# A gated recurrence by products of gates folded level by level, and the first two tiles' merge in its stage

## The reference, cut to what matters

```
def gla_chunk(S, q, k, v, g):
    C = q.shape[2]
    cum = jnp.cumsum(g, axis=2)
    inter = jnp.einsum('bhtc,bhcv->bhtv', q * jnp.exp(cum), S)
    diff = cum[:, :, :, None, :] - cum[:, :, None, :, :]
    decay = jnp.where(causal, jnp.exp(jnp.where(causal, diff, 0.0)), 0.0)
    A = jnp.einsum('bhtc,bhsc,bhtsc->bhts', q, k, decay)
    intra = jnp.einsum('bhts,bhsv->bhtv', A, v)
    last = cum[:, :, -1]
    S_new = (jnp.exp(last)[..., None] * S
             + jnp.einsum('bhsc,bhsv->bhcv', k * jnp.exp(last[:, :, None, :] - cum), v))
    return S_new, inter + intra

q = silu(rq); f = lb + (1 - lb) * sigmoid(rf); k = 1 - f; g = log(f)   # 4 heads, 128 features, 528 tokens
o = rmsnorm(o, norm_w) * silu(rg)
x = x + concat(att, o) @ w_out
```

## Time and profile before

| | us |
|---|---|
| median of three runs | 3038.01 |
| the profiled execution, its own time | 3036.15 |
| its span in the profile | 3034.3 |
| the recurrence, 291.06 to 393.54 | 102.5 |
| the first merge, 393.85 to 440.68 | 46.8 |
| the norm behind it, 441.0 to 454.16 | 13.2 |

### The profile page before, as it was taken

How to read it: one execution, slowest core, us unless ns; L and a number is a source line. 1 busy time by engine, 2 the same in 40 slices (tenths; PEclk the granted TensorE clock), 3 DMA queues, 4 the chain that set the end, 5 groups by cost and what they waited for, 6 DMA issues and landing times. The chain is left out here.

```text
span 3034.3 us, 32474 instructions
## 1 busy us (share of the span) xinstructions
PE 2652.2 (87%) x11426; PEld 1813.3 (60%) x11426; DVE 1893.7 (62%) x3864; ACT 1289.7 (43%) x2806; POOL 669.0 (22%) x638
## 2 busy tenths in 40 slices
PE   6988768898889877789999999699798697999998
PEld 6877647334444332245555555499686455788887
DVE  5786836777777677777777776555554655343323
ACT  3234223544444344555656655344234245232222
POOL 2210000434443433444444434100000020000000
PEclk9998788999999999999999999899898699999999
DMA  6752024999999999999999999656130101222332
GB/s 214 277 183 61 1 97 162 411 413 406 420 420 421 405 404 422 419 412 419 419 412 412 408 415 415 238 186 194 65 94 28 37 22 49 98 70 97 98 99 75
DMA packets 131731, 750.81 MB, mean 247 GB/s; under 512 B 17408, under 2 KB 17936, under 8 KB 65248
## 3 DMA queue, kind: packets, MB, share of 16 engines
q0 software_dynamic: 81824, 575.43, 46.7%
q1 hardware_dynamic: 49744, 173.30, 16.5%
HBM read 746.57 MB, written 2.10 MB: 247 GB/s over the span
## 5 line engine op out<-in xcount | busy, mean ns | idle before, releaser
L1646 PE MATMUL peer_y<-rows,diag 128*128 128x512 f32 x2048 | 995.2, 613 | 178.0 <-ACT diag L1626 166.3
L1600 DVE CUSTOM_DVE_ANT_0 rows<-rows,hidden 128x1024 f32<-128x1024 f32 x512 | 627.8, 1226 | 375.6 <-DMA rows<-in_peer_table,experts 370.4
L1587 POOL DMA_INDIRECT rows<-in_peer_table,experts x512 | 587.8, 1148 | 1042.5 <-PE peer_y L1646 799.2
L1646 PEld LDWEIGHTS peer_y<-rows,diag 128*128 128x128 f32 x2048 | 363.1, 192 | 592.2 <-ACT diag L1626 301.3
L1623 ACT ACTIVATE hid<-hid 128x1 f32<-128x1 f32 x512 | 102.6, 200 | 544.1 <-DVE hid L1600 540.7
L2249 DVE TENSOR_TENSOR piece_w_low<-piece_raw,piece_w_high 128x1024 fp32r<-128x1024 f32 x132 | 161.1, 1222 | 102.4 <-ACT piece_w_high L2244 102.2
L1626 ACT ACTIVATE diag<-ident,hid 128x128 f32<-128x128 f32 x512 | 205.6, 401 | 16.7
L2244 ACT ACTIVATE piece_w_high<-piece_raw 128x1024 fp32r<-128x1024 f32 x132 | 138.6, 1052 | 108.2 <-PE out_bank L152 77.6
L1624 ACT ACTIVATE hid<-hid,gates 128x1 f32<-128x1 f32 x512 | 150.8, 295 | 16.6
L417 ACT ACTIVATE proj_w_high<-proj_raw 128x1024 fp32r<-128x1024 f32 (+2 forms) x57 | 57.5, 1012 | 217.1 <-PE proj_pair L152 116.9
L150 PE MATMUL peer_y<-peer_feat_high,early_w_high 128*128 128x256 f32 x352 | 144.5, 410 | 2.0 <-issue 2.0
(11 more groups left out here) (522 smaller groups left out, 5637.1 us busy)
## 6 DMA issues: line engine op xcount, KB each, us to landing
ada<-in_w_ada POOLq DMA_DIRECT2D x96, 384.0 KB, 4.4
piece_raw<-in_ffn_w_gate SPq DMA_DIRECT2D x44, 512.0 KB, 3.5
piece_raw<-in_ffn_w_up SPq DMA_DIRECT2D x44, 512.0 KB, 4.4
piece_raw<-in_ffn_w_down SPq DMA_DIRECT2D x44, 512.0 KB, 3.4
query_raw<-in_peer_w_query SPq DMA_DIRECT2D x32, 512.0 KB, 6.6
early_raw<-in_ffn_w_gate SPq DMA_DIRECT2D x22, 512.0 KB
early_raw<-in_ffn_w_up SPq DMA_DIRECT2D x22, 512.0 KB, 14.4
early_raw<-in_ffn_w_down SPq DMA_DIRECT2D x22, 512.0 KB, 7.8
```

The lines of the kernel that those rows point to most:

```text
L1587: pool.indirect_dma_start(self.rows[:, b, :], None, self.table, bass.IndirectOffsetOnAxis(ap=self.experts[:, unit % self.SETS, n % TOPK:n ...
L1600: dve.tensor_tensor_reduce(out=self.rows[:, b, 0:D], in0=self.rows[:, b, 0:D], in1=self.hidden[:, tile, :], scale=1.0, scalar=0.0, op0=ALU ...
L1646: last = pe.matmul(self.y[self.bank(tile)][:, c * BANK:(c + 1) * BANK], self.diag[:, b, :], self.rows[:, b, D + c * BANK:D + (c + 1) * BAN ...
```

## The change

`gated_scan` and `first_merge(half=0)` become one stage, `scan_and_merge`.

The gates are no longer turned into logarithms. The levels now go from the finest to the coarsest, and keys and queries are changed in place. Level 0 multiplies keys by plain queries, level 1 keys by queries times their gate; after each further level the second half of each block pair of the queries is multiplied by the product of the gates of the first half (`fold`, on VectorE), and the first half of the keys by the product of the gates of the second (on GpSimd). The products themselves come by halving (`next_gain`). Masks are now "at least so far apart", and a coarser level overwrites a finer one. From level 5 on ScalarE copies the blocks from PSUM without a mask. Tiles go in two chunks of 256 tokens, each with waits of its own. Logarithm, exponentials, running sums, `differences` and `weighted` are gone.

The merge of tiles 0 and 1 follows in the same stage: the attention half's squares, sums, root and scaling stand beside the levels, and `w_out` is loaded at the stage's start. The one-column sums of the modulation and what VectorE makes of them move into `peer_features(half=0)`, as the class `Modulation`.

```
+        qe = room.sbuf("qe", [P, RH, T])
+        gain = [t.fm[:, AH:2 * AH, :]]
+        for j in range(1, LV + 1):
+            gain.append(room.sbuf(f"gain{2 ** j}", [P, RH, (NT if j <= 4 else T) // 2 ** j])[:, :, :])
...
+            pool.wait_ge(keys_ready, 1)
+            for j in range(LV - 1):
+                if j:
+                    pool.wait_ge(gained, j)
+                for c in range(2):
+                    lo, hi = (0 if c == 0 and j <= 3 else NM + c * CHUNK), NM + (c + 1) * CHUNK
+                    own = halves(k[:, :, lo:hi], 2 ** j, False)
+                    back = 0 if j <= 4 else NM
+                    pool.wait_ge(l_done, (j + 1) * TT + 2 * c + 2)
+                    pool.tensor_tensor(own, own, gains(j, lo - back, hi - back, True), ALU.mult).then_inc(folded_keys, 1)
...
+            move_gate(0)
+            move_gate(1)
+            act.wait_ge(ms_ready, 1)
+            act.activation(ss[:, :, 0:4], ss[:, :, 0:4], ACT.Sqrt).then_inc(rstd_ready, 1)
+            for u in range(2, 6):
+                move_gate(u)
+            for n in range(TT):
+                kept(OPEN, n)
             move_keys(0)
+            for c in range(2):
+                kept(LV - 1, 2 * c)
+                kept(LV - 1, 2 * c + 1)
+                last_halves(c)
+            kept(LV, 0)
+            kept(LV, 1)
             move_keys(1)
+            move_keys(2)
+            kept(LV, 2)
+            kept(LV, 3)
+            move_keys(3)
+            for n in range(2):
                 act.wait_ge(o_summed, n + 1)
+                act.activation(t.rec[:, n, :], o_bank[n], ACT.Copy)
+                act.activation(sq[:, n * BANK:(n + 1) * BANK], o_bank[n], ACT.Square).then_inc(squared, 1)
...
+            def fold_queries(j, c):
+                b, lo, hi = 2 ** j, c * CHUNK, (c + 1) * CHUNK
+                own = halves(qe[:, :, lo:hi], b, True)
+                return dve.tensor_tensor(own, own, gains(j, real_at(j) + lo, real_at(j) + hi, False), ALU.mult)
+
+            def fold(j, c):
+                dve.wait_ge(l_done, (j + 1) * TT + 2 * c + 2)
+                fold_queries(j, c).then_inc(folded, 1)
...
+            def next_gain(j):
+
+                own = gain[j][:, :, 1:] if j == 4 else gain[j]
+                two = own.rearrange("p h (m w) -> p h m w", w=2)
+                dve.tensor_tensor(gain[j + 1], two[:, :, :, 0], two[:, :, :, 1], ALU.mult).then_inc(gained, 1)
+                dve.wait_ge(gained, j + 1)
...
+            for lv in range(OPEN):
+                for c in range(2):
+                    kept(lv, 2 * c)
+                    kept(lv, 2 * c + 1)
+                    if lv >= 1:
+                        fold(lv - 1, c)
+                next_gain(lv)
+                if lv == 0:
+                    mean_squares(0)
+                if lv == 1:
+                    dve.wait_ge(rstd_ready, 1)
+                    for i in range(2):
+                        last = normed(0, i)
+                    last.then_inc(scaled, 1)
+            for j in (OPEN - 1, OPEN):
+                for c in range(2):
+                    fold(j, c)
+                    if j == OPEN:
+                        fold_last_keys(c)
+                if j == OPEN - 1:
+                    next_gain(OPEN)
+                    next_gain(OPEN + 1)
+                    next_state(0)
+            for c in range(2):
+                fold_last_queries(c)
+            for m in range(1, TT):
+                next_state(m)
+            mean_squares(1)
...
+            for lv in range(LV):
+                for n in range(TT):
+                    level(lv, n)
+                if lv < 4:
+                    gate_row(2 + lv)
+                if lv == OPEN:
+                    turn_keys(0)
+                    state_sums(0)
+            level(LV, 0)
+            level(LV, 1)
             turn_keys(1)
+            turn_keys(2)
+            level(LV, 2)
+            level(LV, 3)
+            state_sums(1)
+            turn_keys(3)
+            state_sums(2)
+            state_sums(3)
             for n in range(TT):
                 outputs(n)
+            pe.wait_ge(scaled, 3)
...
+class Modulation:
...
+    def sums(self, pe):
+        pe.wait_ge(self.ones_ready, 2)
+        for part, pair_of in enumerate(self.PARTS):
+            for a, m in enumerate(pair_of):
+                for f in range(KC):
+                    col = m * D + f * P
+                    last = pe.matmul(self.cols[:, part, a, f:f + 1], self.t.ada_acc[:, col:col + P], self.ones[:, 0:1],
+                                     start=True, stop=True)
+        last.then_inc(self.done, 1)
...
@@ peer_features, TensorE, behind the four groups of transposes @@
+            if modulation is not None:
+                modulation.sums(pe)
             beside.sums(pe, END)
```

More of the change, by code:

```diff
@@ L1036, in _ @@
-            dve.wait_ge(apart_ready, 1)
-            for lv in range(LV + 1):
-                last = dve.tensor_scalar(inside[:, lv, :], apart[:, :], float(2 * HALVES[lv] if lv < LV else 1), None,
-                                         ALU.is_lt)
-            last.then_inc(masks, 1)
-            dve.wait_ge(logs, 1)
-            chain.link(dve.tensor_scalar(k, k, -1.0, 1.0, ALU.mult, ALU.add))
-            for h in range(RH):
-                last = dve.tensor_tensor_scan(cum[:, h, :], keep[:, :], cum[:, h, :], 0.0, ALU.mult, ALU.add)
-                last.then_inc(cum_done, 1) if h == RH - 1 else chain.link(last)
@@ L1105, in _ @@
[L1105 to L1111 removed]
+            dve.wait_ge(sigmoids, 1)
+            for h in range(RH):
+                last = dve.tensor_scalar(gain[0][:, h, :], t.fm[:, K + h, :], t.one_lb[:, h:h + 1], t.lb[:, h:h + 1],
+                                         ALU.mult, ALU.add)
@@ new lines, in _ @@
+            dve.wait_ge(rstd_ready, 2)
+            dve.wait_ge(gates, 1)
+            for i in range(2):
+                chain.link(normed(1, i))
+                dve.tensor_tensor(t.rec[:, i, :], t.rec[:, i, :], t.rg[:, i, :], ALU.mult).then_inc(scaled, 1)
+            for u in range(4):
+                tile, c = u // 2, u % 2
+                dve.wait_ge(out_done, u + 1)
+                x = t.x[:, tile, c * BANK:(c + 1) * BANK]
+                dve.tensor_tensor(x, x, turn_bank[u], ALU.add)
@@ new lines, in _ @@
+            pe.wait_ge(moved, KC)
+            pe.wait_ge(w_loaded, 32)
+            for u in range(4):
+                i, c = u // 2, u % 2
+                for f in range(KC):
+                    last = pe.matmul(turn_bank[u], feat[:, f, i * P:(i + 1) * P], w_out[:, c, f, :],
+                                     start=(f == 0), stop=(f == KC - 1))
+                last.then_inc(out_done, 1)
+        for name, n in (("squared", 4), ("ms", 2), ("rstd", 2), ("gates", 1), ("scaled", 3), ("turned", 4), ("moved", KC),
+                        ("out_done", 4)):
+            Signal(core, f"merge_{name}").used(n)
@@ L1210, in part_of @@
             return (t.mixed if part == 0 else t.rec)[:, 2 * half + i, :]
-        if half == 0:
-            @block.sync
-            def _(sp):
-                for c in range(2):
-                    sp.dma_start(w_out[:, c, :, :], dram["w_out_t"][c]).then_inc(w_loaded.handle, 16)
         @block.gpsimd
@@ L1303, in _ @@
             beside.sums(pe, END)
-        for s, n in ((w_loaded, 32 * (half == 0)), (squared, 4), (sums, 2), (ms_ready, 1), (rstd_ready, 1), (gates, 1),
+        for s, n in ((squared, 4), (sums, 2), (ms_ready, 1), (rstd_ready, 1), (gates, 1),
                      (scaled, 4), (turned, 4), (moved, KC), (out_done, 4)):
@@ L1386, in _ @@
             beside.dots(dve, END)
+            if modulation is not None:
+                modulation.move(dve, chain)
         @block.tensor
@@ L3272, in half_of @@
                 keys_in = Signal(core, "keys_in")
-                peer_features(core, t, dram, half, half_feat, norm_room, e.hidden, row_w, beside, weights, keys, keys_in)
+                modulation = Modulation(core, t, dram, small, e.y[0]) if half == 0 else None
+                peer_features(core, t, dram, half, half_feat, norm_room, e.hidden, row_w, beside, weights, keys, keys_in,
+                              modulation)
                 peer_scores(core, t, dram, half, half_feat, weights, keys, keys_in, query, scores, beside, e)
```

372 lines of the change are left out of this document (193 added, 179 removed).

## The result

The changed kernel takes 2994.97 us (median of 4 runs, 2991.26 to 2997.85). The kernel before, run beside it on the same chip, takes 3037.48 us. The ratio is 0.9862, with a 95% interval from 0.9847 to 0.9876, so 42.5 us less. Forecast were 2998 us and 40 us less.

A forecast was written before the change was run, and what follows sets the result against it. VectorE's hand-written order was taken to pace the old levels and TensorE the merge, with stages in series. Gain 54.5, less 4 for GpSimd and 10.5 for modulation, gave 40 us less: 2998 us, range 2984 to 3018.

The forecast's parts named there:

- lock included: Levels: GpSimd's folds hold VectorE operations through the shared port pair, 4 us against the gain, bounds 0 and 18.
- the walk: Step-by-step timing of the new recurrence and merge stage on the old profile's clock: ends at 386.2, not 440.7, gain 54.5 us.
- 4 us of held operations: Levels: VectorE's folds, gains and attention-half scalings may wait until GpSimd's folds are through; 4 us against.
- The rival with a low clock throughout: Levels and outputs: TensorE's clock stays low, some 20 us more, 3018 us; chance 0.07.
- The price on VectorE: Levels: GpSimd's folds delay four of ten VectorE folds and one pair of scalings; 4 us, bounds 0 and 18.
- the operations named: Levels: four of VectorE's ten folds and one pair of scalings, hit by 0.3 to 1.4 us each.
- The rival of an exclusive port as the bound: Levels: GpSimd's and VectorE's folds exclude each other, or a fold takes 2.8 us; 3012, with both 3016; chance 0.17.
- the middle value: Merge: passes by `w_out` and last addition take 29.5 us, between 28.7 at full clock and the earlier 30.7.
- The modulation: Norm stage: 96 one-column passes behind the transposes, only 6.8 us covered; 10.5 us against, bounds 4.6 and 14.5.
- The picture of fast passes first and slow ones behind: Norm stage: 40 one-column passes at 0.115 us in 4.6 us, then the clock falls and 56 run at 0.215.
- given back later: Later stages: the gain is lost if one waits for something with a time of its own; chance 0.01.

The follow-up runs named there:

- the folds in part: Changed kernel, but each of GpSimd's twelve key folds multiplies only one block of one head, leaving out nearly all key folding; 2991.13 us, ratio 0.9865 to the kernel before.
- the merge apart: Changed kernel, but the first two tiles' merge is again its own stage behind the recurrence, with the attention half's norm in it; 2997.74 us, ratio 0.9889.

## Why the prediction was right

**The recurrence.** Its outputs were forecast to begin 38.7 us earlier, lock included; it was 39.4 in the mean. The first masked copy came 9.5 us into the stage (forecast 9.8), level 0 was through at 16.6 (16.5). TensorE ended level 5 at 40.3, where the walk's 36.3 and its 4 us of held operations give the same. That is luck in part: 1.6 of it is the low clock in level 3, and in the other two profiles the level ended at 38.7. There the held operations cost 3.7 (35.0 with the folds in part), and the walk without them was 1.3 too long. From there to the outputs it took 15.8 (15.4), which again holds 1.6 us of low clock that the walk didn't have. The copies come 0.65 us apart and a fold takes 0.67, with 0.59 to the next operation, as taken from the earlier trace rows. ScalarE's block copies, estimated between the earlier trace rows, took 0.23, 0.28 and 0.38 us for 0.22, 0.28 and 0.43. Behind level 0 the clock cost more than the nothing put down for it: 1.6 us in the 48 passes of levels 6 and 7, and 1.6 in level 3 in one profile of three. The rival with a low clock throughout is out, as the levels took 0.117 a pass but for the one.

**GpSimd.** A fold was put at 1.5 us between 1.2 and 2.8. It takes 1.11 to 1.21 when nothing holds it, at or under the lower bound, and up to 1.59 when something does. The price on VectorE was put at 4; the kernel with the key folds left out in part shows 3.7 to 4.2. The bounds of 0 and 18 were wide enough to hold nearly anything, but the operations named (four folds and the pair of scalings) are the ones that were held; of what was held, only L1079 with its 1.06 us is of a kind that the prediction didn't name. The rival of an exclusive port as the bound (3012 to 3016) is out: the 16 masked copies took 0.70 to 0.74 us each, with folds beside many of them, and 0.71 to 0.74 before the change with none. The Trainium skill ("SBUF — State Buffer", section "SBUF: two separate sides") says that the later of the two waits for the whole instruction of the other. The trace agrees on both sides. The first scaling started at 311.25 beside a fold that ran from 311.02 to 312.44, and it ended 0.54 us behind the fold where it takes 0.69 by itself. A fold of GpSimd that started at 328.76, just behind one of VectorE that ran from 328.72 to 329.41, ended 0.94 us behind that one where it takes 1.11 by itself.

What the prediction didn't ask is whether GpSimd is worth it. In the changed kernel it hardly is: all folds on VectorE give 2993.69, the same within the spread.

**The merge.** From the outputs to its end 41.9 us (43.3). The passes by `w_out` ran all at the full clock and took 28.5 with the last addition; I had taken the middle value, 29.5.

**The modulation.** This is the term that was too small. Forecast 10.5 us, with bounds of 4.6 (4.8 by its own terms) and 14.5; it cost 13.5, 14.1 and 11.3 in the three profiles, 13.0 in the mean. There are two parts. The passes took 17.8, 18.3 and 15.5 us, where 16.6 were forecast (17.2 in the mean). The picture of fast passes first and slow ones behind is right: clock 0.91 from 396.4 to 400 and 0.50 from there to the end. The other part was missing: the norm's transposes ahead of them took 5.47 us in all three, and not the 3.84 of the earlier trace rows, partly at the low clock after the same 3.7 us of idleness. That is 1.6 of the 2.5 us. They ran in 3.84 before and in three of the experiments' profiles, in 5.47 in four, and in 6.6 in two; why isn't settled.

**The sum.** -39.4 for the recurrence, -13.2 for the merge and +13.0 for the modulation give the -39.7 (-39.6 by the rounded terms), against a forecast of -38.7, -11.8 and +10.5. So the sum is closer than its terms, which is luck: the modulation's 2.5 too little was made up by 0.7 and 1.4 too little gain. The 3 us beyond it are those of the experts' part that no step of the prediction covers. Nothing was given back later: the first gather starts 40 us earlier from the stage's start.

What paid was the algorithm. With the merge apart, the folded recurrence alone begins its outputs 45.2 us earlier than before. The common stage then adds 3 us by the split and 4 by the medians.

## What to carry to other kernels

When an edit removes a long preparation, ask what was hidden under it. Here 20 us of one-column sums had cost nothing, and cost 13 us behind the norm or 15 at the start once their cover was gone; cut up, most of them fit into waits that TensorE had anyway.

In a loop where two engines have nearly the same time for a round, nothing is free to put "beside" it. The attention half's sums and scalings on VectorE cost 5 us in the levels, and nothing measurable behind them. Work handed to GpSimd paid 1.2 us here where VectorE set the pace and was held by it, and 3.5 where the levels went at TensorE's pace with GpSimd's folds and at VectorE's without them. VectorE's folds were held there too (one took 1.63 us), but TensorE's 4.55 us a level hid it.

## What the runs showed of the hardware that was not expected

- A VectorE operation on 8 columns with one tensor input took 1229 ns beside a GpSimd fold and 173 alone. I had looked for holding only in operations with two inputs in SBUF. The same section of the Trainium skill names, beside these, a mode of VectorE that uses both ports; which mode this operation ran in no run here shows. Masked copies out of PSUM were never held (0.70 to 0.74 us).
- The holding goes both ways. GpSimd's folds of 512 elements took 1.11 to 1.15 us beside masked copies and 1.50 to 1.59 when VectorE worked on two SBUF tiles. The Trainium skill ("GPSIMD Engine Reference", section "Elementwise — side-by-side cycle accounting") has 4497 ns for 2048 elements, from which I had estimated 1.2 for a fold of 544. The trace has 1.15 and 1.21 for the ones beside masked copies.
- One-column passes kept TensorE busy from end to end and the granted clock fell under them all the same, from a mean of 0.91 up to 400.0 to 0.50 from there on. In three profiles of one kernel 96 of them took 15.5, 17.8 and 18.3 us. At the stage's start, they took 20.64, as before the change.
- The granted clock also fell to 0.50 and rose again inside the 48 passes of levels 6 and 7, with TensorE busy from end to end. They took 7.25 us in six profiles and 5.62 to 5.82 in three, with the wait of 1.19 us ahead of them in profiles of both kinds. No run here shows what decides it.
